# Last expert round of a decoder trunk: weights in half-width transfers, block stores issued by ScalarE instead of by the sync engine

## What is computed

```python
def _moe_swiglu(h, router_w, router_b, w_gate, w_up, w_down):
    hf = h.reshape(bsz * seq, d)
    logits = (hf @ router_w + router_b).astype(jnp.float32)
    probs = jax.nn.softmax(logits, axis=-1)
    top_p, top_i = lax.top_k(probs, TOP_K)
    top_p = top_p / jnp.sum(top_p, axis=-1, keepdims=True)
    gates = jnp.sum(jax.nn.one_hot(top_i, N_EXPERTS, dtype=jnp.float32) * top_p[..., None], axis=1)
    out = jnp.zeros_like(hf)
    for e in range(N_EXPERTS):
        out = out + gates[:, e:e + 1] * _swiglu(hf, w_gate[e], w_up[e], w_down[e])
    return out.reshape(bsz, seq, d)
```

## Time and profile before

| | |
|---|---|
| runs | 1463.14, 1456.54, 1461.38 us; median 1461.38 |
| profiled execution | 1464.03 us, its span 1462.2 us |
| TensorE busy | 1370.1 us, 94% of the span |
| VectorE, ScalarE, GpSimd busy | 405.6, 150.9, 169.1 us |
| DMA | 499.93 MB, mean 342 GB/s |
| expert weights | 168 transfers of 2048 KB from SP |
| stores of blocks | 19 transfers of 128 KB from SP |

### The profile page before, as it was taken

How to read it: one execution, slowest core, us unless ns; L and a number is a source line. 1 busy time by engine, 2 the same in 40 slices (tenths; PEclk the granted TensorE clock), 3 DMA queues, 4 the chain that set the end, 5 groups by cost and what they waited for, 6 DMA issues and landing times.

```text
span 1462.2 us, 43274 instructions
## 1 busy us (share of the span) xinstructions
PE 1370.1 (94%) x19076; PEld 1046.7 (72%) x19076; DVE 405.6 (28%) x1018; ACT 150.9 (10%) x362; POOL 169.1 (12%) x244
## 2 busy tenths in 40 slices
PE   4999999999998898999999989989989999999984
PEld 3887788888787786766677767757757776766762
DVE  2825251453515616111111111111111111111224
ACT  2202121000003104100000000000000000000001
POOL 0000052351401300000000000000000000000001
PEclk8999999999999999999999999999999999999997
DMA  9947578777467507779999999999999999999984
GB/s 383 422 184 302 232 270 282 273 298 284 171 236 288 203 1 308 326 282 427 426 421 414 427 425 414 427 426 408 427 426 411 418 426 424 417 425 426 407 343 170
DMA packets 52818, 499.93 MB, mean 342 GB/s; under 512 B 6668, under 2 KB 13964, under 8 KB 15372
## 3 DMA queue, kind: packets, MB, share of 16 engines
q1 hardware_dynamic: 45708, 463.36, 77.3%
q10 hardware_dynamic: 6400, 32.39, 5.9%
q0 software_dynamic: 576, 2.10, 0.4%
HBM read 485.38 MB, written 16.58 MB: 343 GB/s over the span
## 4 chain that ended last, share of the span: by engine, by line
PE 74%; DMA 15%; DVE 4%; SPq 3%; issue 1%; ACT 1%; POOL 0%; ACTq 0%; POOLq 0%; DVEq 0%
PE PS L795 29%; PE PS L499 19%; PE PS L804 14%; DMA ring<-in_expert_stream 9%; PE PS L649 4%; SPq L431 2%; DMA arena<-in_mod_rows 2%; DVE arena L1137 2%; DMA arena<-in_expert_stream 2%; DMA ring<-in_dense_stream 2%; PE PS L775 2%; PE PS L483 1%; PE PS L531 1%; PE PS L473 1%; PE PS L703 1%
## 5 line engine op out<-in xcount | busy, mean ns | idle before, releaser
L795 PE MATMUL PS<-ring,arena 128*32 128x256 f32 x8288 | 483.2, 381 | 26.1 <-DMA ring<-in_expert_stream 21.7
L795 PEld LDWEIGHTS PS<-ring,arena 128*32 128x32 f32 x8288 | 313.5, 110 | 164.7 <-DMA ring<-in_expert_stream 19.1
L499 PE MATMUL PS<-arena,ring 128*128 128x256 f32 x1408 | 311.9, 383 | 6.2 <-ACT arena L925 4.6
L499 PEld LDWEIGHTS PS<-arena,ring 128*128 128x128 f32 x1408 | 268.7, 192 | 46.0 <-issue 7.1
L804 PE MATMUL PS<-ring,arena 128*32 128x256 f32 x3456 | 208.6, 379 | 0.0
L1137 DVE TENSOR_TENSOR stat<-stat,PS 128x128 f32<-128x128 f32 x154 | 44.4, 288 | 515.4 <-ACT stat L1088 515.4
L804 PEld LDWEIGHTS PS<-ring,arena 128*32 128x32 f32 x3456 | 130.3, 110 | 56.8 <-issue 0.6
L1750 POOL COPY arena<-arena 128x256 f32 x153 | 61.5, 402 | 791.7 <-PE PS L795 791.7
L1137 DVE TENSOR_TENSOR arena<-arena,PS 128x256 f32 (+1 forms) x142 | 63.3, 446 | 238.6 <-PE PS L804 161.6
L1088 ACT ACTIVATE stat<-PS 128x128 f32<-128x128 f32 x154 | 43.2, 280 | 782.4 <-PE PS L795 782.4
L795 PE MATMUL PS<-arena 128*32 128x256 f32 x1568 | 94.8, 379 | 4.3 <-DMA ring<-in_expert_stream 4.3
(11 more groups left out here) (206 smaller groups left out, 624.6 us busy)
## 6 DMA issues: line engine op xcount, KB each, us to landing
ring<-in_expert_stream SPq DMA_DIRECT2D x133, 2048.0 KB, 21.7
ring<-in_dense_stream SPq DMA_DIRECT2D x91, 1024.0 KB, 9.3
arena<-in_expert_stream SPq DMA_DIRECT2D x35, 2048.0 KB, 20.1
arena<-in_mod_rows ACTq DMA_DIRECT2D x14, 1024.0 KB, 6.5
ssm_scratch<-arena ACTq DMA_DIRECT2D x8, 1024.0 KB, 10.0
ring<-ssm_scratch SPq DMA_DIRECT2D x8, 1024.0 KB, 8.7
ring<-kc_scratch SPq DMA_DIRECT2D x32, 128.0 KB, 2.4
y_scratch<-arena SPq DMA_DIRECT2D x19, 128.0 KB
```

What stands on the lines that cost most here:

```text
L499: mm = pe.matmul(PS[:, bank, j * T:(j + 1) * T], w[:, c, j * P:(j + 1) * P], moving[:, c, :], start=(c == 0), stop=(c == NC - 1))
L795: mm = pe.matmul(PS[32 * q:32 * q + 32, 0, 0:256], hbuf[:, c * BLK:(c + 1) * BLK], w[:, q * 256:(q + 1) * 256], start=(c == 0), stop=(c == ...
```

## The change

In the last round (`n >= HALVED`, the last 24 pairs) each pair is loaded as two transfers of half its columns, 128 x 8 KB, on the same semaphore. SP stores nothing any more. ScalarE's last round becomes three parts: two Silus (`BEHIND`), then a loop over blocks 2 to 20 with a Silu, a wait for `y_scaled` and the store of the block two before, then the last Silu. That is again 19 stores, of blocks 0 to 18. VectorE's first count on `y_scaled` and POOL's count of stores follow.

```diff
-STORED_EARLY = 3
-STORE_FROM = PAIRS - STORED_EARLY * STEP
+BEHIND, FILLS = 2, -(-MOST * BLK // T)
+HALVED = PAIRS - EXPERTS * STEP
...
-            return pair_sem(n), 16 * (dense_uses + sum(PAIR_PLAN[m][0] == s for m in range(n + 1)))
+            return pair_sem(n), 16 * (dense_uses + sum(1 + (m >= HALVED) for m in range(n + 1) if PAIR_PLAN[m][0] == s))
...
             def load_pair(n):
-                sp.dma_start(pair_slot(n), expert_in[n]).then_inc(pair_sem(n), 16)
+                if n < HALVED:
+                    sp.dma_start(pair_slot(n), expert_in[n]).then_inc(pair_sem(n), 16)
+                    return
+                for at in (slice(0, PIECE), slice(PIECE, 2 * PIECE)):
+                    sp.dma_start(pair_slot(n)[:, at], expert_in[n][:, at]).then_inc(pair_sem(n), 16)
...
-                if STORE_FROM - 1 <= n < PAIRS - 1 and n % STEP == GU:
-                    store_rows(upto, (n + 1 - STORE_FROM) // STEP)
-
-            for e in range(STORED_EARLY, LAST_E):
-                store_rows(upto, e)
...
-            for rnd in range(1, ROUNDS):
+            for rnd in range(1, ROUNDS - 1):
                 with act.Fori(0, upto[-1]) as j:
                     act.wait_ge(gu_done, j + upto[-1] * rnd + 1)
                     silu().then_inc(silu_ready, 1)
+            rnd = ROUNDS - 1
+            act.wait_ge(y_stored, 16 * FILLS)
+            with act.Fori(0, BEHIND) as j:
+                act.wait_ge(gu_done, j + upto[-1] * rnd + 1)
+                silu().then_inc(silu_ready, 1)
+            with act.Fori(BEHIND, upto[-1] - 1) as j:
+                act.wait_ge(gu_done, j + upto[-1] * rnd + 1)
+                silu().then_inc(silu_ready, 1)
+                act.wait_ge(y_scaled, j)
+                act.dma_start(y_scr[bass.ds(j * BLK - BEHIND * BLK, BLK), :].rearrange("i (q n) -> q i n", q=4),
+                              acc[:, bass.ds(j * 256 - BEHIND * 256, 256)]).then_inc(y_stored, 16)
+            act.wait_ge(gu_done, upto[-1] * ROUNDS)
+            silu().then_inc(silu_ready, 1)
...
-            dve.nop().then_inc(y_scaled, 1)
+            dve.nop().then_inc(y_scaled, BEHIND - 1)
...
-            pool.wait_ge(y_stored, upto[LAST_E - 1] * 16 + 16 * (FILLS - 1))
+            pool.wait_ge(y_stored, upto[-1] * 16 + 16 * (FILLS - BEHIND - 1))
```

More of the change, by code:

```diff
@@ L150 @@
 LAST_E = EXPERTS - 1
-FILLS = -(-MOST * BLK // T)
-STORED_EARLY = 3
-STORE_FROM = PAIRS - STORED_EARLY * STEP
+BEHIND, FILLS = 2, -(-MOST * BLK // T)
+HALVED = PAIRS - EXPERTS * STEP
+assert FILLS > BEHIND + 1
 FREE_AT = Y_PAIR // STEP % EXPERTS
@@ L423, in _ @@
                 load_pair(n)
[L425 to L432, removed]
             sp.wait_ge(items_ready, 1)
```

## The result

| | before | changed |
|---|---|---|
| median, us | 1461.31 (1456.54 to 1463.14, 4 runs) | 1479.36 (1471.27 to 1482.54, 4 runs) |
| ratio | 1 | 1.0116, 95% interval 1.0088 to 1.0143 |
| profiled execution, us (span) | 1464.0 (1462.2) | 1471.27 (1469.4) |

The changed kernel is slower, by 1.2%. A second series on another occasion gave 1474.76 us (1470.1 to 1476.46, 4 runs) against 1461.89, ratio 1.0079 (1.0051 to 1.0107). The median of its eight runs is 1476.0; 1477 was forecast. The first profile shows the second fastest of the eight executions, so the round is read here from two profiles.

A forecast was written before the change was run, and what follows sets the result against it. Four DMA engines, full with weights and stores (85 us of work in 85), were taken to set the last store's end. Blocked ScalarE issues +18.5, tail -2.7, sum +15.8 us on 1461.4: 1477; range 1459 to 1482 plus 1.

The forecast's parts named there:

- Time, sign and mechanism: Last expert round: stores wait behind weights, blocked issues stop ScalarE and delay Silus; slower, 1477 us, chance 0.67.
- Row for row in turn: DMA engines: one ScalarE store row per SP weight row, 32 turns or 11.4 us a store against 5.18 a block.
- case C: Rival: stores pass quickly in turns of many rows, nothing blocks, last weights land later; +6, 1467.5 us, chance 0.10.
- Three stores held: ScalarE's DMA queue holds three waiting stores and the fourth issue is blocked; bounds two (1482 us) and four (1472).
- Half-width loads, +2 us: Last round's 24 weight pairs: rows of 8 KB move slower than rows of 16 KB; 2 us taken, 0 to 3.4 kept.
- Silu 21 at +18.5 us: Last block's Silu comes at 1455.1 against 1436.63, as ScalarE stands at store 14 until the last weights land near 1433.
- the stores pile up as long as weights are queued, and they are nearly all the time: ScalarE's queue from block 2 on: stores accumulate beside nearly continuous weights; 11 done and 14 accepted near 1433.
- The tail, -2.7: After the last block: stored rows are gathered while TensorE finishes, so VectorE's four sums follow directly, 2.7 us earlier.
- The sum: Whole kernel: +18.5 us on the last Silu less 2.7 in the tail gives +15.8, forecast 1477 us.
- Rival D: Last round: weight loads go out earlier, stores hide, TensorE's and the tail's waits go; -10.3, 1451 us, chance 0.08.

The follow-up runs named there:

- experiment 3: Changed kernel with each store issued as four transfers of 32 partitions, 8 rows on each of 16 DMA engines: 1454.79 us, ratio 0.9951 to the kernel before.
- Experiment 2: Changed kernel with the last round's weights in full width again (16 KB rows), stores still on ScalarE: 1485.28 us, ratio 1.0168 to the kernel before.
- experiment 6: Changed kernel with each store as two transfers of 16 rows on each of the same four engines: 1477.51 us, ratio 1.0106 to the kernel before.
- experiment 8: Changed kernel with stores spread over 16 engines from ScalarE and weights whole: 1448.96 us, ratio 0.9921 to the kernel before; median of twelve runs 1450.0.
- experiment 1: Kernel before with only its last round's weights in half-width transfers, stores still on SP: 1463.18 us, ratio 1.0008.
- experiment 9: Changed kernel with the 19 four-engine stores issued by GpSimd between its loads of blocks: 1487.58 us, ratio 1.0172 to the kernel before.
- 4: Changed kernel storing only 64 of each block's 128 rows, 16 on each of the four engines: 1459.38 us, ratio 0.9986 to the kernel before.
- 7: Kernel before with each store as four transfers over all 16 engines, still on SP, weights whole: 1459.43 us, ratio 0.9985.
- 8's second: Unaltered repeat of the changed kernel with 16-engine stores on ScalarE and whole weights: 1451.06 us, ratio 0.9941 to the kernel before.
- 10's second: Kernel with 16-engine ScalarE stores and whole weights, GpSimd also waiting for block 20's scatter before the gathers: 1453.63 us, against 1451.06 without that wait.
- 10's first: Changed kernel with 16-engine stores, GpSimd also waiting for the last e_down before the gathers: 1455.00 us, ratio 0.9954 to the kernel before.

## Why the forecast held, step by step

**Time, sign and mechanism: right.** ScalarE's issues are blocked from block 7 on, as the forecast put it, and the Silus, VectorE's products and TensorE follow. The timeline shows each Silu late behind its blocked issue, and experiment 3 agrees: rows per engine cut to a quarter, no issue blocked, 21 us gone.

**Row for row in turn: right, its price a tenth too high.** A turn was put at 0.357 us and is 0.314; a store has 33 turns where 32 were counted, so it takes 10.3 us instead of 11.4. Experiment 2's 19.0 us (forecast 21) is off by the same tenth. The forecast gave the weight row its time with all 16 engines equally loaded; in the mix all 16 stay full (420 to 422 GB/s) while twelve of them see no store rows. That this makes the difference isn't shown. The small stores of the earlier trace rows agree in kind. The Trainium skill ("DMA: Bandwidth & Descriptors", "Queues, rings and completion order") lets an engine drain a packet of typically 9 to 17 descriptors before it turns (two to four packets to a store, where the forecast says two or three turns). The counts alone don't refute that, since equal packets on both sides would give the same mean pace, but the starts do: in 1400 to 1420 the 255 packets of ScalarE's queue start no more than 0.15 us apart, and in each 0.32 us three to six of them, about one for each of the four engines. Were nine rows drained at a time, an engine would start no store row for some 2.5 us in between (an estimate, nine weight rows of 0.28 us), and the four together would leave longer gaps than that 0.15. So here the turn is one row, and case C, which had nothing blocked, didn't come about.

**Three stores held: right for the blocked issues, not a fixed count.** The first blocked issue returned with 3.0 and 3.1 stores left in the two profiles (394 and 410 packets, 132 to a store), 2.9 in experiment 6. But the seventeenth store of the changed kernel was accepted in 0.9 us with 4.2 left, and experiment 2's sixth in 0.58 us with as many. What goes with the blocking is rows, not transfers (experiments 6 and 8).

**Half-width loads, +2 us: right**, +0.9 in experiment 1's profile between Silu -2 and Silu 21 (134.7 against 133.8), at most 0.2% in its ratio.

**Silu 21 at +18.5 us: too much; it is +10.9 and +10.2.** The step that failed is "the stores pile up as long as weights are queued, and they are nearly all the time". The last pair landed where it was put: at 1429.2, which is 1434 on the clock of the kernel before (4.8 us later into the round), against 1433. But ScalarE stood behind Silu 18 by then (1427.92) and not behind Silu 16. It had issued 17 stores, of which 12.8 had passed, and not 14 and 11. The missing turn of thought: a blocked ScalarE also holds back the experts, the experts their slots, and the slots the loads. SP issued no load from 1359.7 to 1375.5, a gap of 16 us where experiment 3 has one of 8 at the same loads. So the weights' queue ran dry at 1373, and 3.3 stores went by at 1.4 us each (the 442 packets above). That is also why the blocked issues come in two groups of three, 49 us apart, and not in one row.

**The tail, -2.7: wrong, +1.1 and +1.3.** The stores were in, and the gathers were no longer waited for, as the step said: VectorE's four sums run without a gap from 1457.85. What failed is the premise that TensorE's last blocks would run as they did before. The gathers now fall together with TensorE's last blocks, and VectorE hears of `e_down` late:
```profile
1442.17 1.17 POOL L1775 DMA_INDIRECT arena<-y_scratch,slots_i  x1 [4.07 <-POOLq L1770]
...
1442.48 1.94 PE L795 MATMUL PS<-arena 128*32 128x256 f32 x32
...
1447.82 0.31 DVE L1571 STREAM_TRANSPOSE arena<-stat 128x128 f32<-128x128 f32 x1 [4.48 <-remote]
...
1448.69 3.55 PE L795 MATMUL PS<-arena 128*32 128x256 f32 x32 [3.20 <-DVE consts L1141]
```
The `e_down` ended at 1444.4, and VectorE's transpose starts at 1447.8, where 0.1 us is usual. Then TensorE's next matmuls take 3.55 us instead of 1.93. It had stood for 3.2 us, and the window row shows its granted clock at 0.50, the lower of its levels (1.2 GHz):
```profile
1448.70:1450.50 1.80, 1.80 (x20) 0.99 (x24) 1.51 (x4) 0.00 (x0) 0.00 (x0) 0.50 0.88 314
```
Where no completion was late (experiment 8's first profile, and experiment 9) Silu 21 to the end takes 21.7 us, 3.9 less than before. So there was a gain to be had, larger than said, and the late completion with what follows it took 5 us.

**The sum.** +10.9 + 1.1 = +12.0 and +10.2 + 1.3 = +11.5 in the two profiles, against +15.8 by the forecast. On the median of the kernel before this gives 1473; the eight runs' median is 1476.0. The 3 us between lie ahead of the round or in the spread of the runs, which no profile settles. That the forecast came within 1 us of the median is luck in part: 8 us too much on the Silus stand against 4 too little in the tail and these 3.

**Rival D, faster, had hold of something.** It was costed at -10.3 us, and refused because the four engines were full. With the rows spread over 16, the stores cost each engine a quarter of the 26 us (an estimate, 6.5), and experiment 8 is at -11. The figure agrees; that its 11 us are D's terms isn't shown.

## What to carry to other kernels

Before you move DMA issues to a computing engine, count the rows that each DMA engine gets, and how many turns beside a bulk queue they need: if that takes longer than the engine's loop, its queue fills and the engine stops with it. Here 32 rows on four engines needed 10.3 us against a block's 5.2, and the issues blocked; 8 rows on sixteen passed in some 4 us beside weight rows of 8 KB, and in 6.8 us beside rows of 16 KB, where the queue grew but the round ended before it blocked. Two edits may each be worth nothing or less alone and 11 us together, so try the spread and the move as a pair.

## What the runs showed that was not expected

- **A full queue goes by rows an engine, not by transfers.** ScalarE's blocked issues returned with 87 to 113 packets an engine left in its queue, whether these were 3 transfers or 5.8, and 17 transfers of 3 packets an engine were accepted without a block. Nor is it bytes: SP issued three pairs of 2 MB in 2.2 us. But up to 140 packets an engine were accepted at once in other places, so the limit itself stays open.
- **TensorE's completions are late while gathers are issued.** A completion that VectorE waited for was on time when it fell up to 0.8 us, or 4.3 us and more, behind the first gather's start (experiment 8's first profile, experiment 9). In the nine other profiles in which one fell from 1.1 to 4.0 us behind it (the changed kernel twice, 2, 3, 4, 6, 7, 8's second, 10's second) it was heard 1.0 to 3.6 us late, never later than 6.1 us behind that start. In the kernel before, in 1 and in 10's first one falls there too, but VectorE waits longer for a gather. 10's second run moved one into that stretch on purpose. The cause isn't shown, only that the lateness goes with the place of the gathers.
- **More and smaller transfers cost ScalarE little.** One transfer of 32 partitions took 0.33 us of ScalarE, one of 128 partitions 0.58, so four cost 1.9 us with their gaps, hidden in the 4.9 us that it waits per block.
